# Merge gates projected inside the attention stage, four products per unit, and no longer inside the delta rule

## The reference, cut to what matters

```python
def _mixer(h, w_in, ...):
    proj = h @ w_in
    ...
    qkv_a, z_a, beta_a, alpha_a, q_b, k_b, v_b, gate_a, gate_b = jnp.split(proj, split_points, axis=-1)
    o_a = _deltanet_branch(qkv_a, z_a, beta_a, alpha_a, a_log, dt_bias, conv_w, gn_w)
    o_b = _neighbourhood_attention(q_b, k_b, v_b, rpb)
    merged = jax.nn.sigmoid(gate_a) * (o_a @ w_oa) + jax.nn.sigmoid(gate_b) * (o_b @ w_ob)
    return merged @ w_out
```

## Time and profile before

| what | us |
|---|---|
| median of 3 runs | 2832.91 (2812.67 to 2837.86) |
| the profiled execution | 2837.16, its span 2835.4 |
| mean granted TensorE clock of it | 0.938 |

### The profile page before, as it was taken

The page is one execution under the profiler, slowest core; times in us unless marked ns, Lnnn a source line. Parts: engine busy times, 40 slices in busy tenths (PEclk is TensorE's granted clock), DMA queues, the critical chain, the costliest instruction groups (busy, mean ns, idle before and its releaser), DMA issues. The chain is left out here.

```text
span 2835.4 us, 32777 instructions
## 1 busy us (share of the span) xinstructions
PE 2648.7 (93%) x11148; PEld 1771.3 (62%) x11148; DVE 1575.7 (56%) x1868; ACT 1177.4 (42%) x1392; POOL 451.4 (16%) x373
## 2 busy tenths in 40 slices
PE   7999999999999997899889859999999999999994
PEld 2465546646564654566334448888888888888883
DVE  2343334434343442344121168888888888888884
ACT  2222121212212221444111137777767776666773
POOL 2022020202110220100122310111111111111101
PEclk9999999999999999555899969999999999999997
DMA  6112301120221111700722169999999999999994
GB/s 209 45 40 65 91 15 60 34 86 19 71 57 49 50 55 40 144 22 0 230 67 111 69 220 357 374 375 373 375 375 374 372 376 377 375 372 378 374 376 163
DMA packets 266085, 539.72 MB, mean 190 GB/s; under 512 B 12297, under 2 KB 65646, under 8 KB 265998
## 3 DMA queue, kind: packets, MB, share of 16 engines
q1 hardware_dynamic: 250125, 498.63, 49.7%
q0 software_dynamic: 4608, 16.78, 2.3%
q10 hardware_dynamic: 11264, 23.14, 2.3%
HBM read 502.82 MB, written 35.68 MB: 190 GB/s over the span
## 5 line engine op out<-in xcount | busy, mean ns | idle before, releaser
L1867 PE MATMUL ps<-whigh,xeT 128*128 128x512 f32 x2048 | 669.1, 400 | 9.2 <-DVE xeT L2012 9.2
L2020 DVE TENSOR_TENSOR wlow<-hT,whigh 128x2048 fp32r<-128x2048 f32 x192 | 432.0, 2284 | 84.7 <-ACT whigh L1963 84.7
L705 PE MATMUL ps<-hT,obT 128*128 128x512 f32 x896 | 442.5, 607 | 17.3 <-ACT obT L884 17.3
L1867 PEld LDWEIGHTS ps<-whigh,xeT 128*128 128x128 f32 x2048 | 387.0, 189 | 100.2 <-issue 9.5
L1867 PE MATMUL ps<-wlow,xeT 128*128 128x512 f32 x1024 | 406.6, 397 | 0.0
L1963 ACT ACTIVATE whigh<-hT 128x2048 fp32r<-128x2048 f32 x192 | 358.5, 1910 | 17.9 <-PE ps L1867 17.9
L1867 PE MATMUL ps<-whigh,hidT 128*128 128x512 f32 x1024 | 334.6, 398 | 1.5 <-DVE hidT L2047 1.5
L2020 DVE TENSOR_TENSOR wlow<-oaT,whigh 128x2048 fp32r<-128x2048 f32 x96 | 216.8, 2286 | 50.2 <-ACT whigh L1963 50.2
L2020 DVE TENSOR_TENSOR wlow<-obT,whigh 128x2048 fp32r<-128x2048 f32 x96 | 217.9, 2284 | 29.6 <-ACT whigh L1963 29.6
L705 PEld LDWEIGHTS ps<-hT,obT 128*128 128x128 f32 x896 | 149.2, 190 | 136.1 <-issue 94.9
L721 PE MATMUL ps<-hT,w 128*128 128x512 f32 x512 | 222.5, 596 | 6.9 <-DVE oaT L1074 3.9
(11 more groups left out here) (271 smaller groups left out, 3283.8 us busy)
## 6 DMA issues: line engine op xcount, KB each, us to landing
hT<-in_w_down SPq DMA_DIRECT2D x66, 1024.0 KB, 8.9
obT<-in_w_up SPq DMA_DIRECT2D x64, 1024.0 KB, 8.8
hT<-in_w_up SPq DMA_DIRECT2D x64, 1024.0 KB, 6.5
hT<-in_w_gate SPq DMA_DIRECT2D x62, 1024.0 KB, 9.3
oaT<-in_w_down SPq DMA_DIRECT2D x62, 1024.0 KB, 6.9
oaT<-in_w_gate SPq DMA_DIRECT2D x34, 1024.0 KB, 9.0
obT<-in_w_gate SPq DMA_DIRECT2D x32, 1024.0 KB, 6.5
ada_d<-in_w_ada SPq DMA_DIRECT2D x8, 2048.0 KB, 9.9
```

Source lines behind the costliest of these rows:

```text
L705: mm = pe.matmul(ps[:, 2, :], we[i % 2][:, k, :], m["hT"][:, k, u * SEQ:(u + 1) * SEQ], start=(k == 0), stop=(k == KD - 1))
L1867: mm = pe.matmul(out, lhs[x], rhs[y], start=start and i == 0, stop=stop and i == 2)
L2020: dve.tensor_tensor(wlow[slot][:, :], raw[(FIRST + x) % RAW_SLOTS], whigh[slot][:, :].bitcast(F32), ALU.subtract).then_inc(low_done, 1)
```

## The change

The 16 gate tiles leave the delta rule. `ETILES` is 3 instead of 7: 24 products a pass instead of 56. The fills become 2, 2, 0, 0, (0, 2), one in each level instead of two, 1 before the modulation row instead of 5, one in each of seven scan steps instead of two, and 5 at the end instead of 7. ScalarE keeps three units a pass instead of seven.

In the attention, PE makes four gate products behind each of the 16 units' other work (`gates(PER_SLOT)`), from weight tiles `wg` (two buffers, loaded by SP) and `hT`, in PSUM bank 1. ScalarE copies a unit behind the exponential of every second w and stores it (`keep_gate`). The v and output transposes of both groups share bank 0, the second group's v transposed one unit later. ScalarE waits for its stores at the end of a turn. The load of x into `hT` moves from SP in the attention to ScalarE's queue in the merge stage, ahead of the sigmoids.

```diff
-    ETILES = EARLY_TILES // HA
+    ETILES = GATE_TILE // HA
...
-FILL = (0, 1)
+FILL = (1, 1, 1, 1, 1)
+FILL_SCAN = (0, 1, 1, 1, 1, 1, 1, 1)
...
                 for d in range(2):
                     pe.matmul(ps[:, d, :], m["ones"][:, :], gsum[d][:, :, :], start=True,
                               stop=True).then_inc(row_ps[d], 1)
-                fill(4)
+                fill(2)
...
                     for t in range(TPG):
                         mm = pe.transpose(ps[:, 6 + i, t * P:(t + 1) * P], src[:, t, :], ident)
                     mm.then_inc(chn_ps, 1)
-                fill(4)
+                fill(2)
...
                         mm = pe.matmul(ps[:, 3 + i, t * P:(t + 1) * P], lhs[:, t, :], knT[:, t, :],
                                        start=True, stop=True)
                 mm.then_inc(gram_ps, 1)
-                fill(1)
...
                     for t in range(TPG):
                         mm = pe.transpose(ps[:, 5 + d, t * P:(t + 1) * P], qe[d][:, t, :], ident)
                     mm.then_inc(qeT_ps, 1)
-                fill(3)
                 for d in range(2):
...
                     for t in range(TPG):
                         mm = pe.transpose(ps[:, 5 + 2 * d, t * P:(t + 1) * P], dec[d][:, t, :], ident)
                     mm.then_inc(xT_ps[d], 1)
-                    fill((2, 6)[d])
+                    fill((0, 2)[d])
...
                             for t in range(TPG):
                                 mm = pe.transpose(ps[:, 5 + 2 * d, t * P:(t + 1) * P], inv[d][:, 0, t, :], ident)
                             mm.then_inc(invT_ps[d], 1)
-                    fill(FILL[d])
+                    fill(FILL[lv])
                     for d in range(2):
...
                                 mm = pe.matmul(ps[:, 5 + 2 * d, t * P:(t + 1) * P], xb[d][:, t, :], inv[d][:, 1, t, :],
                                                start=True, stop=True)
                         mm.then_inc(upd_ps[d], 1)
-                    fill(FILL[d])
                 for d in range(2):
...
                         mm = pe.matmul(ps[:, 4 + 2 * d, t * P:(t + 1) * P], kbe[d][:, t, :], inv[d][:, 1, t, :],
                                        start=True, stop=True)
                     mm.then_inc(uw_ps[d], 1)
-                fill(5)
+                fill(1)
...
                             pe.wait_ge(state_done[d], n * NC1 + i)
                             pe.matmul(ps[rows, 5 + 2 * d, 0:P], xbT[d][:, t, rows],
                                       state[d][:, i, :], start=True, stop=True).then_inc(ws_ps[d], 1)
-                    if i > 0:
-                        fill(FILL[d])
+                    fill(FILL_SCAN[i])
                     for d in range(2):
...
                         if i < NC1:
                             pe.matmul(ps[:, 5 + 2 * d, P:2 * P], kd[d][rows, t, :], vnew[d][rows, t, :],
                                       start=True, stop=True).then_inc(kv_ps[d], 1)
-                    if i < NC1:
-                        fill(FILL[d])
                 pe.wait_ge(mod_done, n + 1)
...
                                   state[d][:, chunks(d).index(c), :], start=False, stop=False)
                     mm = pe.matmul(out, qkT[1][:, t, :], vnew[1][:, t, :], start=False, stop=True)
                 mm.then_inc(o_ps, 1)
-                fill(7)
+                fill(5)
                 pe.wait_ge(on_done, 1 + n + 1)
...
                     act.wait_ge(chn_ps, 2 * n + i + 1)
                     act.activation(dst[:, :, :], ps[:, 6 + i, :], ACT.Copy).then_inc(chn_sb, 1)
-                keep_early()
                 for d in range(2):
...
                     act.wait_ge(xT_ps[d], 2 * n + 2)
                     act.activation(qkT[d][:, :, :], ps[:, 5 + 2 * d, :], ACT.Copy).then_inc(xT_sb[d], 1)
-                keep_early()
                 for lv in range(1, LV):
...
                     act.activation(vnew[d][:, :, :], ps[:, d, :], ACT.Copy).then_inc(uw_sb[d], 1)
                     act.activation(xbT[d][:, :, :], ps[:, 4 + 2 * d, :], ACT.Copy).then_inc(uw_sb[d], 1)
-                for _ in range(3):
-                    keep_early()
+                keep_early()
                 act.wait_ge(o_ps, n + 1)
...
     NU = GROUPS * 2 * TPG
+    GTILES = 2 * KD // PAIRS
+    GUNITS = GTILES * GROUPS
+    PER_SLOT = GUNITS * KD // NU
...
+wg = [sb(f"wg{i}", [P, KD, P]) for i in range(2)]
+gst = [sb(f"gst{g}", [P, SEQ]) for g in range(GROUPS)]
...
+        w_in = a["w_in"].rearrange("a (k p) n -> p (a k) n", p=P)
         load_rel(0, 2, rel_first)
...
         sp.dma_start(raw[:, :, :].unsqueeze(2), early_v[:, :, 0:1, :]).then_inc(raw_in, 16)
+        for i in range(2):
+            sp.dma_start(wg[i][:, :, :], w_in[:, :, OFF_GA + i * P:OFF_GA + (i + 1) * P]).then_inc(wg_in[i], 16)
         load_rel(2, HB, rel_in)
-        sp.dma_start(m["hT"][:, :, :], a["x"].rearrange("(t p) c -> p t c", p=P)).then_inc(x_in, 16)
+        def next_weights(h, i):
...
+            sp.wait_ge(gate_ps, 1 + h * GUNITS + GROUPS * (i + 1))
+            sp.dma_start(wg[i % 2][:, :, :], w_in[:, :, bass.ds(h * (GTILES * P) + (OFF_GA + (i + 2) * P), P)]).then_inc(
+                wg_in[i % 2], 16)
...
         with sp.Fori(0, PAIRS - 1) as h:
...
             sp.dma_start(raw[:, :, :].unsqueeze(2), early_v[:, :, 1:, :][:, :, bass.ds(h, 1), :]).then_inc(raw_in, 16)
+            for i in range(GTILES):
+                next_weights(h, i)
+        for i in range(GTILES - 2):
+            next_weights(PAIRS - 1, i)
...
         ident = m["ident"][:, :]
-        prime(pe, pT_ps, pv_ps)
+        prime(pe, pT_ps, pv_ps, gate_ps)
         with pe.Fori(0, PAIRS) as h:
-            def turn_v():
...
-                pe.wait_ge(ob_done, 1 + h * GROUPS)
-                for g in range(GROUPS):
-                    pe.wait_ge(take_done, h * NPROJ + (5 + g))
-                    for t in range(TPG):
-                        mm = pe.transpose(ps[:, g, t * P:(t + 1) * P], vT[:, g, t * P:(t + 1) * P], ident)
-                    mm.then_inc(vt_ps, 1)
+            products = iter(range(GUNITS * KD))
...
+            def gates(count):
...
+                for _ in range(count):
+                    unit, k = divmod(next(products), KD)
+                    i, u = divmod(unit, GROUPS)
+                    if k == 0:
+                        pe.wait_ge(wg_in[i % 2], h * (16 * GTILES // 2) + 16 * (i // 2 + 1))
+                        pe.wait_ge(gate_sb, 1 + h * GUNITS + unit)
+                    mm = pe.matmul(ps[:, 1, :], wg[i % 2][:, k, :], m["hT"][:, k, u * SEQ:(u + 1) * SEQ],
+                                   start=(k == 0), stop=(k == KD - 1))
+                    if k == KD - 1:
+                        mm.then_inc(gate_ps, 1)
...
+            def turn_v(g):
...
+                if g == 0:
+                    pe.wait_ge(ob_done, 1 + h * GROUPS)
+                else:
+                    pe.wait_ge(vtok_sb, h * GROUPS + 1)
+                pe.wait_ge(take_done, h * NPROJ + (5 + g))
+                for t in range(TPG):
+                    mm = pe.transpose(ps[:, 0, t * P:(t + 1) * P], vT[:, g, t * P:(t + 1) * P], ident)
+                mm.then_inc(vt_ps, 1)
...
                     scores(w)
-                if w == 1:
-                    turn_v()
+                if w in (1, 2):
+                    turn_v(w - 1)
                 if 2 <= w < NU + 2:
...
                     values(w - 3)
+                if w < NU:
+                    gates(PER_SLOT)
             for g in range(GROUPS):
                 pe.wait_ge(otok_done, 1 + h * NU + (g + 1) * 2 * TPG)
-                pe.wait_ge(ob_done, 1 + h * GROUPS)
+                pe.wait_ge(ob_done, 1 + h * GROUPS + g)
                 for t in range(TPG):
-                    mm = pe.transpose(ps[:, g, t * P:(t + 1) * P], otok[:, g, t, :], ident)
+                    mm = pe.transpose(ps[:, 0, t * P:(t + 1) * P], otok[:, g, t, :], ident)
                 mm.then_inc(obT_ps, 1)
...
     def _(act):
+        gates_v = early_dram[GATE_TILE * P:, :].rearrange("(j p) t -> p j t", p=P)
         with act.Fori(0, PAIRS) as h:
+            def keep_gate(unit):
...
+                i, u = divmod(unit, GROUPS)
+                act.wait_ge(gate_ps, 1 + h * GUNITS + (unit + 1))
+                if i >= 1:
+                    act.wait_ge(gate_out[u], h * (16 * GTILES) + 16 * i)
+                act.activation(gst[u][:, :], ps[:, 1, :], ACT.Copy).then_inc(gate_sb, 1)
+                act.wait_ge(gate_sb, 1 + h * GUNITS + (unit + 1))
+                act.dma_start(gates_v[:, bass.ds(h * GTILES + i, 1), u * SEQ:(u + 1) * SEQ],
+                              gst[u][:, :].unsqueeze(1)).then_inc(gate_out[u], 16)
...
                                scale=(-DH ** -0.5 if b == 0 else 1.0)).then_inc(take_done, 1)
-            for g in range(GROUPS):
-                act.wait_ge(vt_ps, h * GROUPS + (g + 1))
-                act.activation(vtok[:, g, :, :], ps[:, g, :], ACT.Copy).then_inc(vtok_sb, 1)
```

(11 more changed lines are left out.)

15 lines of the change are left out of this document (10 added, 5 removed).

## The result

The changed kernel takes 2912.4 us (median of 4 runs, 2910.4 to 2914.9), the kernel before 2833.1 beside it: ratio 1.030, 95% interval 1.025 to 1.035. The forecast was 2865, range 2832 to 2905: right in its sign, 47 us too low, and outside its own range.

| stretch | before | after | difference | forecast |
|---|---|---|---|---|
| delta rule, to the last transposes of `on` | 1116.95 | 1031.57 | -85.4 | -109 |
| from there to attention's first scores | 23.4 | 21.7 | -1.7 | 0 |
| attention, first scores to the last copy of obT | 209.8 | 365.5 | +155.7 | +138 |
| merge, from there to the first product of the route | 137.1 | 147.3 | +10.2 | +4 |
| the rest | 1348.1 | 1346.8 | -1.3 | 0 |

A forecast was written before the change was run, and what follows sets the result against it. PE was taken to bound the delta rule at full clock and to run attention at half. Delta rule -128, its clock +19, attention +138 and merge +4 gave +33 us, median 2832.9 to about 2865, range 2832 to 2905.

The forecast's parts named there:

- PE's clock would rise in attention: Attention loop: the moved gate products raise PE from clock 0.50 to 1.00; attention costs +138 us in all.
- the part to the first inverse level: Delta rule pass, up to the first level: 14 products (12.0 us) go, GpSimd's chain then rules, 3.85 us gained.
- the 4.5 us behind L814: Delta rule pass, between levels and scan: 10.72 us becomes 6.24 with one fill left, 4.5 us gained.
- the clock falls in the wait for GpSimd: Delta rule, before the second L785: PE's gap of some 4.3 us halves the clock, 2.4 us a pass, +19 us.
- The scan step: Delta rule's scan: seven steps of 2.45 us with one fill each, 3.9 us gained of 7.4 a pass.
- the levels: Delta rule's inverse levels: five products fewer, VectorE then binds at 5.98 us a level, 2.1 us gained of 4.3.
- the full 1.7: End of a delta rule pass: two of seven fills go and their whole 1.7 us is gained.
- The prediction's own five terms: PE work of an attention unit: gates 3.43, scores 0.53, transposes 0.28, values 0.60, tile turn 0.2; together 4.94 to 5.0 us.
- the 79.0 us for a turn: Attention turn through its last gate slot at full clock: gates, scores, tile turns, transposes, values and v, 79.0 us.
- The tail between the last gate and the next scores: End of an attention turn: ScalarE's copy, store landing (2.0) and three rearranged copies take 6.5 us, three times.
- weights arriving late: Merge stage, with x loaded on ScalarE's queue: 3 us of the merge term of +4 us.
- The first rival: The clock holds: no loss in the delta rule, attention turns lose 2 instead of 8; 2840 us, chance 0.27.

The follow-up runs named there:

- `end_fills`: Changed kernel, but each head's second pass has seven fills at its end instead of five and none in the last two scan steps; 2905.5 us (1.025).
- `warm_hold_5`: Kernel before plus 22 useless PE products ahead of attention's first turn, five at every turn's start, x loaded on SP's queue at merge's end; 2760.7 us (0.974).
- `store_wait`: Changed kernel, but ScalarE waits for a gate store only before writing that staging tile again, not at the turn's end; 2900.2 us (1.023).
- `repaired`: As `store_wait`, also with x loaded on SP's queue behind the merge stage's last weights; 2888.7 us (1.020).
- `one_per_unit_x_late`: Changed kernel with one gate product per unit (8 fills leave each pass), the wait of `store_wait`, x behind merge's last weights on SP's queue; 2768.6 us (0.978).
- `one_per_unit_hold`: `one_per_unit_x_late` plus 20 useless warming products ahead of attention's first turn and two at each turn's start; 2769.3 us (0.978).

## Why the prediction was wrong

Three of its terms were too hopeful: the delta rule by 24 us, attention by 18 and the merge by 6. The two stretches that it put at nothing gave 3 back.

**What held.** That PE's clock would rise in attention; that the part to the first inverse level gives 3.85 us of 12 (3.93: 4.53 to 2.81 and 6.10 to 3.89 in the two stretches around); the 4.5 us behind L814 (10.72 to 6.44, 4.3); that the clock falls in the wait for GpSimd. The eight passes together lose 2.5 us each to it, 20 for the 19 forecast, though not always at the place named.

**Delta rule, 24 us too hopeful.** At full clock, summed from the stretches that no fall touches, a pass went from 101.0 to 86.7 us, 14.3 gained instead of 16.05: 14 us over eight passes. Two terms were mis-sized. The scan step was put at 2.45 us and is 2.60: the state product of both directions starts 0.92 behind L844 and lasts 0.62, where I let it end at 1.4. And the levels gave 1.5 us, not 2.1: VectorE's 5.98 us was counted too short, a level is 6.15 with PE waiting 0.43 for its mask. The other 8.5 us are a step that was wrong in kind: "the full 1.7" for the two fills at a pass's end. In a head's second pass, three times, they stood in the 5 us between `on` and the next head's projections, which don't shrink; their absence became idle time (5.6 us in three head starts) and, at one of them, half clock (57.9 us of projections for 55.0). `end_fills` gives 7 us of it back.

**Attention, 18 us too cheap.** The terms of a turn were right in kind. A unit is 5.15 us (1202.92 to 1223.52, four units). The prediction's own five terms for it add up to 5.04, not to 4.94 to 5.0; the 79.0 us for a turn is right as a sum, for the first units have no transposes and values. The term that was too small is the four gate products, 3.43 us, which take 3.53 to 3.58 between the small products; why isn't shown. Through its sixteenth gate slot a turn takes 83.1 to 83.4 us for 79.0 and 2.1 of half clock: some 9 us in four turns. The tail between the last gate and the next scores is 8.6 to 8.95 us for 6.5: the landing of the last store was sized at 2.0 us from the earlier trace rows and took 4.4, beside the 512 KB that the same product releases: a transfer that the change adds and that the prediction didn't put beside the store. That is 7 us in three turns. The tail of the last turn is 6.2 us for 5.

**Merge, 6 us too cheap.** The prediction looked at the sigmoids, the wait of the earlier trace rows, and gave 3 us for "weights arriving late". The sigmoids moved by 1 us. The weight tiles of the second round, on another queue, stood behind x for 10.

**A row that was read wrongly.** The first rival, that the clock holds, rested on the 1.4 us gap of the earlier trace rows, through which it "held". It held there for some 3.5 us. The rows behind it, of the kernel before:

```profile
1298.41:1299.70 1.29, 1.29 (x4) 0.67 (x4) 0.53 (x2) 1.29 (x2) 0.00 (x0) 1.00 0.00 0
1302.00:1345.00 43.00, 43.00 (x137) 29.16 (x138) 18.36 (x55) 17.25 (x48) 0.00 (x0) 0.50 0.00 0
```

They show the clock back at half for the rest of the turn, so this gap spoke against that rival.

**The frame of the comparison.** The prediction called attention's engine "one that has room, if its clock rises", and measured the gates against today's 51.8 us turn at half clock. The sum needs that, since it compares with the kernel before; but it hides what the gates cost. The experiments put the floor of that turn at 31.2 us at full clock (32.9 in `warm_hold_5`, with its extra products). From there a turn of after is 31.2 and 64 products: 86.2 us at 0.86 each, 88.5 at 0.895. `store_wait` and `repaired` have 86.2 to 90. So no product was ever hidden in attention; each was paid in full, and what the first sixteen seemed to hide was bought by the clock that they held up. In the delta rule the last sixteen of 32 products were nearly free, in part because the clock fell without them. The change moved 256 products from a place where three quarters of them cost 0.1 to 0.4 us each to one where all cost 0.86. The terms for a turn were worked out at full clock, and so came near; what was missing is the question what a turn without gates takes at that clock. It would have shown that the attention stage was slow by its clock and not by its work.

**The best kernel.** `warm_hold_5` at 2760.7 us beats both, by 2.6% and 5.2%, without moving any gate; `one_per_unit_x_late` at 2768.6 does it with work that is needed. The two draw on the same gain, the clock of attention, and `one_per_unit_hold` (2769.3) shows that they hardly add.

## What to carry to other kernels

Before moving work to a stage because its engine runs at half clock, ask what the stage takes at full clock: the work will raise the clock and pay full price from that floor, and a few products that only keep the engine busy may bring the clock alone. Take away filling work step by step, from where it stands on the path, and stop where the next wait binds: here 8 products of 32 carried 6.9 of 11.8 us. And a fill in front of a loop's turn may cover the turn itself.
